# Score matmuls of two heads as 64-row tiles, issued alternately, in place of zero-padded queries

## The chip, the cores and the metric

The kernel runs on one core of a Trainium2 chip. Its time is the device time of one execution, in microseconds (us). A core has five engines that run their own instruction streams and meet at semaphores: TensorE (PE, matrix multiplication, with weight loads shown as PEld), VectorE (DVE), ScalarE (ACT), GpSimd (POOL) and SyncE (SP, here for issuing DMAs). Matmuls write to PSUM, which has 8 banks of 512 float32 columns on 128 partitions.

## The reference, cut to what matters

One layer of a streaming encoder with 1024 prompt tokens and 32 sample tokens: a mixing sub-layer of two head groups, then a SwiGLU feed-forward. The change lies in the mixing sub-layer, in the three places where 64-element queries meet 64-element keys:

```python
# indexer: H_IDX = 8 heads of D_IDX = 64, one shared key
idx = jax.nn.relu(jnp.einsum('bthd,bsd->bths', qi, ki))
score = jnp.einsum('bth,bths->bts', wi, idx)
_, sel = lax.top_k(score, topk)                      # 256 keys per query
# mixer A (band) and mixer B (selected keys): 8 heads of 64
logits = jnp.einsum('bnqhd,bnkhd->bnhqk', q, k) * HEAD_DIM ** -0.5
p = jax.nn.softmax(logits + bias, axis=-1)           # masked
o = jnp.einsum('bnhqk,bnkhd->bnqhd', p, v)
```

Mixer A sees its own chunk and 8 chunks before it (up to 640 keys for a block of 128 queries), mixer B all admissible keys (up to 1024, the sample 1056), of which the indexer's 256 best count. All of it is float32.

## The kernel before, in words

The program is a row of stages, each a block of five engine streams with a barrier behind it: conditioning, projections, `indexer`, `attention(band=True)` (mixer A), `attention(band=False)` (mixer B, with the output projection), then the feed-forward. The change touches `indexer` and the two `attention` stages. In each of them the work is cut into units (t, h): a row block t of 128 queries (t = 0 to 7; t = 8 is the sample with 32 queries) and a head h. A unit's index is u, and in `attention` the program goes by steps s, with unit s scored in step s.

Queries and keys lie transposed, two heads to a tile of 128 partitions: head h has partitions 0 to 63 when h is even, 64 to 127 when it is odd. Keys shared by heads (indexer, mixer B) lie there twice, in both halves. Before the change a score matmul contracts over all 128 partitions. So that the other head adds nothing, POOL copies each unit's query into one of four slots whose other half is zero (`clear_pads`, `fill_pad`, L699), and PE waits for it (`pad_ready`).

`indexer`: PE writes a unit's scores to one of two bank groups (L753) once the unit two before it has been read (L748); ACT applies the relu (L763); DVE multiplies by the head's weight and adds up (L773, L776), and after the last head takes minimum and maximum of the row (L781, L782).

`attention`: in step s PE scores unit s into one of two column ranges of PSUM (L918), once unit s-2 has been masked (L914). DVE adds the near bias (mixer B, L1102) and the mask or band bias with a running minimum (L1110, which raises `masked`); ACT exponentiates (L1001). Two or three steps later PE transposes the weights (L933, a group "T" of up to four blocks) and multiplies with the values (L905, "PV"), reading T's results after ACT or DVE has copied them (L976). When a row block is done, DVE divides by the sums (L1131, at step 8t+8+LAG), PE turns the result (L943, "O"), and in mixer B multiplies with the output weights in two halves of 8 matmuls (L952, "W", at steps 8t+15 and 8t+16); DVE copies W's result (L989), scales it (L1138, at step 8t+19), and POOL adds the residual and stores it (L1163, L1167, L1171). Each engine does its work in program order, so POOL's copies of later queries stand behind its residual work. Beside this DVE carries the search for the top 256: in mixer A a bisection over 24 rounds with counting on DVE (L1063) and ACT (L1011), in mixer B the selection of row block s//8 + 3 in six parts (L1073 to L1085) at steps up to 47.

Of the kernel before, what the change touches and what calls it, by code (L numbers as in the profile page):

```python
# [31 lines left out]
P = 128  # L32
# [4 lines left out]
SAMPLE = NT - 1  # L37
# [44 lines left out]
def rows_of(t):  # L82
    return DEC if t == SAMPLE else P
# [597 lines left out]
def pad_slot(pad, u):  # L681


    return pad + 256 * (u % 2) + P * (u // 2 % 2)


def clear_pads(nc, pool, T, pad, ready):
    nc.gpsimd.memset(T(pad, 256, HD, HD), 0.0).then_inc(ready, 1)
    pool.wait_ge(ready, 1)
    nc.gpsimd.memset(T(pad + 256, 256, HD, 0), 0.0).then_inc(ready, 1)  # L690
    pool.wait_ge(ready, 2)


def fill_pad(nc, pool, T, pad, u, q_at, t, h, used, ready):

    if u >= 4:
        pool.wait_ge(used, u - 3)
    p0, r = HD * (h % 2), rows_of(t)
    nc.gpsimd.tensor_copy(T(pad_slot(pad, u), r, HD, p0), T(q_at + NTOK * (h // 2) + P * t, r, HD, p0)).then_inc(ready, 1)  # L699


def indexer(ctx, nc, ins, outs, sem, T, T3, B, view, ident, d_strip_a, d_strip_b, **_):
# [4 lines left out]
    pad, pad_ready = HT + 7168, sem("pad_ready_i")  # L707
    v_in = sem("v_in")
    EARLY = 24

    def bank(u):
        return 3 * (u % 2)

    with nc.Block() as block:
# [10 lines left out]
        @block.gpsimd  # L725
        def _(pool):
            clear_pads(nc, pool, T, pad, pad_ready)
            for u, (t, h) in enumerate(units[:EARLY]):
                fill_pad(nc, pool, T, pad, u, QI, t, h, idx_mm, pad_ready)
# [10 lines left out]
            for u, (t, h) in enumerate(units[EARLY:], EARLY):  # L740
                fill_pad(nc, pool, T, pad, u, QI, t, h, idx_mm, pad_ready)

        @block.tensor
        def _(pe):
            for u, (t, h) in enumerate(units):
                r = rows_of(t)
                if u >= 2:
                    pe.wait_ge(relu_done, u - 1)  # L748
                pe.wait_ge(pad_ready, u + 3)
                q = T(pad_slot(pad, u), r)  # L750
                for lo, hi in pieces(0, width_b(t), 512):
                    k = T((KI if t < SAMPLE else KIC if lo < PAST else KI + SEQ - PAST) + lo, hi - lo)
                    mm = nc.tensor.matmul(B(bank(u), hi - lo, r, c0=lo), q, k, start=True, stop=True)  # L753
                mm.then_inc(idx_mm, 1)
# [41 lines left out]
def attention(band, ctx, nc, ins, outs, sem, T, T3, B, view, ident, d_ada, d_y, **_):  # L796
# [35 lines left out]
    def key_source(t, h, lo, hi):  # L832

        if band:
            if t == SAMPLE:
                return T(KAC + 512 * (h // 2) + lo, hi - lo) if lo < WIN else T(KA + NTOK * (h // 2) + SEQ + lo - WIN, hi - lo)
            return T(KA + NTOK * (h // 2) + first_key(t) + lo, hi - lo)
        g = h // 4
        if t == SAMPLE:
            return T(KBC + 1024 * g + lo, hi - lo) if lo < PAST else T(KB + NTOK * g + SEQ + lo - PAST, hi - lo)  # L840
        return T(KB + NTOK * g + lo, hi - lo)
# [14 lines left out]

    def s_col(u):
        return 0 if units[u][0] == SAMPLE and not band else 1024 * (u % 2)

    pad = QI + 3168 if band else NAT  # L860
    pad_ready = sem(f"pad_ready_{n}")
# [11 lines left out]
    with nc.Block() as block:  # L873
# [17 lines left out]
        def _(pe):  # L891
# [17 lines left out]
            for s in range(steps):  # L909
                if s < NU:  # L910
                    t, h = units[s]
                    r = rows_of(t)
                    if s >= 2:
                        pe.wait_ge(masked, s if (t == SAMPLE and not band) else s - 1)  # L914
                    pe.wait_ge(pad_ready, s + 3)
                    q = T(pad_slot(pad, s), r)
                    for lo, hi in pieces(0, width(t), 512):
                        mm = nc.tensor.matmul(ps_cols(B, s_col(s) + lo, hi - lo, r), q, key_source(t, h, lo, hi),  # L918
                                              start=True, stop=True)
                    mm.then_inc(qk_mm, 1)  # L920
# [229 lines left out]
        def _(pool):  # L1150
            clear_pads(nc, pool, T, pad, pad_ready)
            for s in range(steps):
                if s < NU:
                    t, h = units[s]
                    fill_pad(nc, pool, T, pad, s, q_at, t, h, qk_mm, pad_ready)
                if band:
                    continue
                for t in range(NT):
                    r = rows_of(t)
                    if s == 8 * t + 8 + 13:  # L1160
                        pool.wait_ge(pad_ready, min(s + 1, NU) + 2)
# [10 lines left out]
            if band:  # L1172
                return
# [380 lines left out]
```

## Time and profile before

| | |
|---|---|
| three timed runs | 1932.95 us median (1930.91 to 1933.37) |
| profiled execution, span of its instructions | 1930.9 us |
| PE busy | 1774.0 us (92%), 9641 matmul records |
| DVE busy | 819.3 us (42%) |
| ACT busy | 651.9 us (34%) |
| POOL busy | 139.4 us (7%) |

The span of the profiled execution equals the lowest of the three runs to a tenth of a microsecond, and lies 2.0 us under their median. Shares of a whole span mix stages with different limits. The stages that the change touches are 435 to 515 us (indexer), 515 to 701 us (mixer A) and 701 to 1071 us (mixer B) of the span; the feed-forward behind them is most of what is left.

### The profile page before, as it was taken

What the parts mean: (1) busy time and instruction counts of PE and PEld (TensorE: products, weight loads), DVE (VectorE), ACT (ScalarE), POOL (GpSimd) and SP (SyncE); (2) the same over time, 40 slices, a digit from 0 to 9 for tenths busy, and PEclk for the clock granted to TensorE, in tenths of its full rate; (3) what the DMA queues carried; (4) which work ended last, traced back from release to release, by engine and by line L of the source; (5) the groups of instructions that cost most, each with busy time, mean ns of one, the idle gap of its engine ahead of it and who ended that gap; (6) DMA issues with size and microseconds to landing.
All of it is one profiled execution on the core that took longest, in us unless ns stands there. A gap on an engine that the chain in (4) does not pass through costs nothing. (4 is left out here: it accounts for less than half of the span.)

```text
span 1930.9 us, 24858 instructions
## 1 busy us (share of the span) xinstructions
PE 1774.0 (92%) x9641; PEld 1436.4 (74%) x9641; DVE 819.3 (42%) x1606; ACT 651.9 (34%) x1188; POOL 139.4 (7%) x273
## 2 busy tenths in 40 slices
PE   7989799999889988899999399999999998999994
PEld 1145499994357865566654299999999998999994
DVE  0120166668899985455433411111111112444446
ACT  1010145545699953233322411111111111333332
POOL 1100000005211011111101100000000000000000
PEclk9999899999899979989999699999999998999997
DMA  9944531113000030000000311111111113200005
GB/s 344 302 80 50 157 77 44 45 35 110 1 1 1 2 134 22 22 22 23 23 23 25 114 56 43 43 44 54 43 43 43 45 42 148 92 0 0 0 0 204
DMA packets 98951, 123.44 MB, mean 64 GB/s; under 512 B 11402, under 2 KB 70866, under 8 KB 98838
## 3 DMA queue, kind: packets, MB, share of 16 engines
q1 hardware_dynamic: 96892, 116.88, 19.8%
q0 software_dynamic: 1984, 5.57, 0.9%
q8 instruction: 46, 0.75, 0.2%
q14 instruction: 29, 0.24, 0.0%
HBM read 105.44 MB, written 18.96 MB: 64 GB/s over the span
## 5 line engine op out<-in xcount | busy, mean ns | idle before, releaser
L1309 PE MATMUL ps<-h_hi,gu_hi 128*128 128x352 f32 x1056 | 341.7, 324 | 8.0 <-DVE gu_lo L1345 8.0
L1309 PE MATMUL ps<-h_lo,gu_hi 128*128 128x352 f32 x1056 | 339.3, 321 | 0.0
L1309 PE MATMUL ps<-h_hi,gu_lo 128*128 128x352 f32 x1056 | 338.9, 321 | 0.0
L918 PE MATMUL ps<-arena 128*128 128x512 f32 (+5 forms) x464 | 181.3, 508 | 35.6 <-DVE small L1110 18.2
L1309 PEld LDWEIGHTS ps<-h_hi,gu_hi 128*128 128x128 f32 x1056 | 198.8, 188 | 8.1 <-DVE gu_lo L1345 8.1
L1309 PEld LDWEIGHTS ps<-h_lo,gu_hi 128*128 128x128 f32 x1056 | 199.1, 189 | 0.0
L1309 PEld LDWEIGHTS ps<-h_hi,gu_lo 128*128 128x128 f32 x1056 | 198.5, 188 | 0.0
L1398 PE MATMUL ps<-a_hi,wd_hi 128*128 128x352 f32 x528 | 174.1, 330 | 13.9 <-DVE a_lo L1421 13.9
L905 PE MATMUL ps<-arena 128*128 128x64 f32 (+2 forms) x1280 | 165.8, 267 | 7.6 <-DVE arena L976 3.2
L1398 PE MATMUL ps<-a_lo,wd_hi 128*128 128x352 f32 x528 | 171.9, 326 | 0.0
L1398 PE MATMUL ps<-a_hi,wd_lo 128*128 128x352 f32 x528 | 171.4, 325 | 0.0
L905 PEld LDWEIGHTS ps<-arena 128*128 128x128 f32 (+2 forms) x1280 | 154.3, 186 | 11.9 <-DVE arena L976 3.6
L918 PEld LDWEIGHTS ps<-arena 128*128 128x128 f32 (+1 forms) x464 | 78.2, 194 | 99.7 <-issue 66.2
L1418 DVE TENSOR_TENSOR wd_lo<-w_down_all,wd_hi 128x1024 fp32r<-128x1024 f32 x66 | 80.8, 1225 | 147.2 <-ACT wd_hi L1410 147.2
L604 PE MATMUL ps<-ht_hi,wb_hi 128*128 128x352 f32 x384 | 128.7, 335 | 12.1 <-DVE ht_lo L641 12.1
L1001 ACT ACTIVATE arena<-arena,small 128x640 f32<-128x640 f32 (+9 forms) x144 | 108.6, 754 | 66.4 <-DVE small L1110 65.9
L1410 ACT CAST wd_hi<-w_down_all 128x1024 fp32r<-128x1024 f32 x66 | 69.1, 1047 | 183.4 <-PE ps L1398 168.0
L952 PE MATMUL ps<-arena 128*128 128x512 f32 (+1 forms) x288 | 127.4, 596 | 0.4 <-ACT arena L983 0.4
L1345 DVE TENSOR_TENSOR gu_lo<-gate_raw,gu_hi 128x1024 fp32r<-128x1024 f32 x22 | 26.9, 1225 | 233.5 <-ACT gu_hi L1323 233.5
L604 PE MATMUL ps<-ht_lo,wb_hi 128*128 128x352 f32 x384 | 125.2, 326 | 0.0
L604 PE MATMUL ps<-ht_hi,wb_lo 128*128 128x352 f32 x384 | 124.8, 325 | 0.0
L976 ACT COPY arena<-ps 128x512 f32<-128x512 f32 (+3 forms) x144 | 66.7, 463 | 169.1 <-PE ps L933 169.0
(172 smaller groups left out, 2611.7 us busy)
## 6 DMA issues: line engine op xcount, KB each, us to landing
arena<-in_w_ada SPq DMA_DIRECT2D x12, 2048.0 KB, 14.0
gate_raw<-in_w_gate SPq DMA_DIRECT2D x22, 512.0 KB, 3.6
up_raw<-in_w_up SPq DMA_DIRECT2D x22, 512.0 KB, 3.7
arena<-in_w_in SPq DMA_DIRECT2D x16, 512.0 KB, 3.5
hidden<-scratch_y SPq DMA_DIRECT2D x4, 2048.0 KB, 12.2
w_down_all<-in_w_down SPq DMA_DIRECT2D x3, 2560.0 KB, 23.6
arena<-in_x_prompt SPq DMA_DIRECT2D x4, 1024.0 KB, 16.1
arena<-in_w_out SPq DMA_DIRECT2D x2, 2048.0 KB, 10.9
```

The costliest lines, as they stand in the source:

```text
L604: mm = nc.tensor.matmul(B(3 * i + c, CH), w_cut[s % 2][a][:, P * i:P * i + P], h_cut[s % 2][b][:, CH * c:CH * c + CH], start=(k == 0 and n ...
L905: mm = nc.tensor.matmul(B(7, HD, r, c0=HD * h), T(pts[t_seq[q] % 4] + P * i, r, k), value_source(t, h, b), start=(b == 0), stop=(b == bloc ...
L918: mm = nc.tensor.matmul(ps_cols(B, s_col(s) + lo, hi - lo, r), q, key_source(t, h, lo, hi), start=True, stop=True)
L952: mm = nc.tensor.matmul(B(bank, 512, r), o, T(W_OUT[c] + 512 * half, 512), start=(c == 0), stop=(c == 7))
L976: copy(view(dst, [[P, len(full)], [1, r]]), view(src, [[P, len(full)], [1, r]])).then_inc(done, 1)
L1001: nc.scalar.activation(T(pbuf[u % NBUF], w, r), T(pbuf[u % NBUF], w, r), ACT.Exp, bias=T(R_NM + u % 16, 1, r), scale=-1.0, accum_out=T(R_S ...
L1309: mm = nc.tensor.matmul(B(3 * i + c, CH), cut[i][a][:, P * k:P * k + P], h[:, NTOK * k + CH * c:NTOK * k + CH * (c + 1)], start=(k == 0 an ...
L1345: nc.vector.tensor_tensor(cut[i][1][:, :], raw[i][:, :], cut[i][0][:, :].bitcast(F32), ALU.subtract).then_inc(cut_lo[i], 1)
L1398: mm = nc.tensor.matmul(B(m, CH), w_cut[k % 2][a][:, P * m:P * m + P], a_cut[k % 2][b][:, :], start=(k == 0 and n == 0), stop=(k == FT - 1 ...
L1410: nc.scalar.copy(w_cut[k % 2][0][:, :], wd[:, D * k:D * k + D]).then_inc(cut_hi, 1)
L1418: nc.vector.tensor_tensor(w_cut[k % 2][1][:, :], wd[:, D * k:D * k + D], w_cut[k % 2][0][:, :].bitcast(F32), ALU.subtract)
```

## The change

POOL's zero-padded slots go. A score matmul contracts over the 64 partitions of its own head, straight from the projected queries. Two heads (h and h+1, one in each half of the partitions) are issued together, one piece of at most 512 columns of the one, then the same piece of the other. The waits change with it: in the indexer a pair has one of two bank groups of 4 banks (for the sample, whose units are wider than 2 banks, a pair waits until every earlier unit is read); in `attention` a pair waits until every earlier unit is masked. The sample of mixer B fills its PSUM columns alone and stays single (`alone`).

```diff
-def clear_pads(...), def fill_pad(...), def pad_slot(...)
+def half_of(h):
+    return HD * (h % 2)
 # indexer
     def bank(u):
-        return 3 * (u % 2)
+        return 3 * (u % 2) if units[u][0] == SAMPLE else 2 * (u % 4)
...
         @block.tensor
-            for u, (t, h) in enumerate(units):
-                if u >= 2:
-                    pe.wait_ge(relu_done, u - 1)
-                pe.wait_ge(pad_ready, u + 3)
-                q = T(pad_slot(pad, u), r)
-                for lo, hi in pieces(0, width_b(t), 512):
-                    mm = nc.tensor.matmul(B(bank(u), hi - lo, r, c0=lo), q, k, start=True, stop=True)
-                mm.then_inc(idx_mm, 1)
+            for u in range(0, len(units), 2):
+                t, h = units[u]
+                if t == SAMPLE:
+                    pe.wait_ge(relu_done, u)
+                elif u >= 4:
+                    pe.wait_ge(relu_done, u - 2)
+                for lo, hi in pieces(0, w, 512):
+                    at = (KI if t < SAMPLE else KIC if lo < PAST else KI + SEQ - PAST) + lo
+                    for i in range(2):
+                        p0 = half_of(h + i)
+                        mm = nc.tensor.matmul(B(bank(u + i), hi - lo, r, c0=lo),
+                                              T(QI + NTOK * (h // 2) + P * t, r, HD, p0), T(at, hi - lo, HD, p0), start=True, stop=True)
+                        if hi == w:
+                            mm.then_inc(idx_mm, 1)
 # attention
+    def alone(u):
+        return units[u][0] == SAMPLE and not band
...
-                if s < NU:
-                    if s >= 2:
-                        pe.wait_ge(masked, s if (t == SAMPLE and not band) else s - 1)
-                    pe.wait_ge(pad_ready, s + 3)
-                    q = T(pad_slot(pad, s), r)
-                    for lo, hi in pieces(0, width(t), 512):
-                        mm = nc.tensor.matmul(ps_cols(B, s_col(s) + lo, hi - lo, r), q, key_source(t, h, lo, hi),
-                                              start=True, stop=True)
-                    mm.then_inc(qk_mm, 1)
+                if s < NU and (alone(s) or s % 2 == 0):
+                    if s:
+                        pe.wait_ge(masked, s)
+                    for lo, hi in pieces(0, w, 512):
+                        for i in range(1 if alone(s) else 2):
+                            q = T(q_at + NTOK * (h // 2) + P * t, r, HD, half_of(h + i))
+                            mm = nc.tensor.matmul(ps_cols(B, s_col(s + i) + lo, hi - lo, r), q, key_source(t, h + i, lo, hi),
+                                                  start=True, stop=True)
+                            if hi == w:
+                                mm.then_inc(qk_mm, 1)
...
         @block.gpsimd
-            clear_pads(nc, pool, T, pad, pad_ready)
+            if band:
+                return
             for s in range(steps):
-                if s < NU:
-                    fill_pad(nc, pool, T, pad, s, q_at, t, h, qk_mm, pad_ready)
                 for t in range(NT):
                     if s == 8 * t + 8 + 13:
-                        pool.wait_ge(pad_ready, min(s + 1, NU) + 2)
                         pool.wait_ge(varm, t + 1)
```

PE in mixer B, row block t = 3 (512 keys), two steps and the start of the third, before (L918 scores, L933 transposes T, L905 values PV):

```order
1966 L918 MATMUL ps<-arena 128x512 [waits pad_ready_b,masked_b]
1967 L933 MATMUL ps<-small,arena 128x128 [waits exp_b,ring_act_b]
1968 L933 MATMUL ps<-small,arena 128x128 x3
1969 L905 MATMUL ps<-arena 128x64 [waits ring_act_b]
1970 L905 MATMUL ps<-arena 128x64 x2
1971 L918 MATMUL ps<-arena 128x512 [waits pad_ready_b,masked_b]
1972 L933 MATMUL ps<-small,arena 128x128 [waits exp_b,ring_dve_b]
1973 L933 MATMUL ps<-small,arena 128x128 x3
1974 L905 MATMUL ps<-arena 128x64 [waits ring_act_b]
1975 L905 MATMUL ps<-arena 128x64 x2
1976 L918 MATMUL ps<-arena 128x512 [waits pad_ready_b,masked_b]
```

The same place after the change (L906 scores, L922 T, L893 PV):

```order
1924 L906 MATMUL ps<-arena 128x512 [waits masked_b]
1925 L906 MATMUL ps<-arena 128x512
1926 L922 MATMUL ps<-small,arena 128x128 [waits exp_b,ring_act_b]
1927 L922 MATMUL ps<-small,arena 128x128 x3
1928 L893 MATMUL ps<-arena 128x64 [waits ring_act_b]
1929 L893 MATMUL ps<-arena 128x64 x2
1930 L922 MATMUL ps<-small,arena 128x128 [waits exp_b,ring_dve_b]
1931 L922 MATMUL ps<-small,arena 128x128 x3
1932 L893 MATMUL ps<-arena 128x64 [waits ring_act_b]
1933 L893 MATMUL ps<-arena 128x64 x2
1934 L906 MATMUL ps<-arena 128x512 [waits masked_b]
1935 L906 MATMUL ps<-arena 128x512
```

The second head's score matmul has moved ahead of one T and PV group, and one wait for the masks stands where two stood. POOL in mixer B, from its copies of queries to the second row block's residual, before:

```order
53 L699 COPY arena<-arena 64x128 [waits qk_mm_b] x18
54 L1163 TENSOR_TENSOR small<-small 128x1 [waits varm,pad_ready_b]
55 L1167 TENSOR_TENSOR arena<-arena 128x1024 [waits xb_in0,m_scaled,rm]
56 L699 COPY arena<-arena 64x128 [waits qk_mm_b,y_done]
57 L699 COPY arena<-arena 64x128 [waits qk_mm_b]
58 L1171 DMA scratch_y<-arena 128x1024 [waits ssy]
59 L699 COPY arena<-arena 64x128 [waits qk_mm_b] x6
```

And after:

```order
34 L1147 TENSOR_TENSOR small<-small 128x1 [waits varm]
35 L1151 TENSOR_TENSOR arena<-arena 128x1024 [waits xb_in0,m_scaled,rm]
36 L1155 DMA scratch_y<-arena 128x1024 [waits ssy,y_done]
37 L1147 TENSOR_TENSOR small<-small 128x1 [waits varm]
38 L1151 TENSOR_TENSOR arena<-arena 128x1024 [waits xb_in1,m_scaled,rm]
```

No copy for PE stands behind POOL's residual work any more.

## Rows read from the trace of the kernel before

**Rows 1.** Stretches of indexer, mixer A, mixer B: length, busy PE, PEld, DVE, ACT, POOL (instructions), clock
```profile
434.90:515.00 80.10, 73.93 (x208) 32.64 (x208) 65.95 (x77) 44.64 (x56) 34.07 (x62) 0.97 0.19 66
515.00:701.00 186.00, 168.82 (x1100) 129.47 (x1100) 166.88 (x597) 166.40 (x370) 20.87 (x74) 0.93 0.00 1
701.00:1071.00 370.00, 341.32 (x1644) 214.08 (x1644) 179.36 (x368) 118.71 (x259) 59.51 (x100) 0.94 0.11 38
```
**Rows 2.** Timeline of the indexer's sample: start, us, engine, line, operation
```profile
497.77 0.11 PEld L753 LDWEIGHTS ps<-arena 128*32 128x32 f32 x1 [0.32 <-issue]
498.20 0.11 PEld L753 LDWEIGHTS ps<-arena 128*32 128x32 f32 x1 [0.32 <-issue]
```
**Rows 3.** Groups by line, DVE, indexer: busy us, mean ns, idle before
```profile
L776 DVE SCALAR_TENSOR_TENSOR tail_attention<-tail_attention,small 128x384 f32<-128x384 f32 (+6 forms) x49 | 49.3, 1006 | 10.0 <-ACT tail_attention L763 6.5
```
**Rows 4.** Groups by line and form, whole span: the indexer's relu and weighting for the sample
```profile
L763 ACT ACTIVATE tail_attention<-ps 32x1056 f32<-32x1056 f32 x8 | 8.3, 1039 | 6.1 <-PE ps L753 5.2 <-DVE tail_attention L773 0.9
L776 DVE SCALAR_TENSOR_TENSOR tail_attention<-tail_attention,small 32x1056 f32<-32x1056 f32 x7 | 9.1, 1306 | 2.1 <-ACT tail_attention L763 1.8
```
**Rows 5.** Timeline of the indexer's start and end
```profile
436.03 4.42 PE L753 MATMUL ps<-arena 128*128 128x384 f32 x8 [2.77 <-POOL arena L699]
438.24 0.42 DVE L773 TENSOR_SCALAR tail_attention<-tail_attention,small 128x384 f32<-128x384 f32 x1 [3.09 <-ACT tail_attention L763]
513.58 1.23 DVE L782 TENSOR_REDUCE small<-tail_attention 32x1 f32<-32x1056 f32 x1
```
**Rows 6.** Groups by line, DVE, mixer A: the copies that wait for PE
```profile
L976 DVE COPY arena<-ps 128x128 f32<-128x128 f32 x32 | 9.2, 288 | 4.2 <-PE ps L933 4.0
```
**Rows 7.** A stretch of mixer A with 640 keys, columns as in Rows 1
```profile
600.00:650.00 50.00, 49.89 (x352) 40.87 (x351) 45.46 (x155) 46.25 (x94) 5.22 (x18) 1.00 0.00 1
```
**Rows 8.** Waits in mixer B from 726 us: total us, times, longest
```profile
PE ps L918 <- POOL arena L699: 9.3, 4, 3.9
```
**Rows 9.** Timeline of mixer B, row block 2, units 21 and 22
```profile
752.54 3.00 POOL L1167 TENSOR_TENSOR arena<-arena 128x1024 f32<-128x1024 f32 x1 [1.45 <-issue]
756.39 0.43 DVE L1102 TENSOR_TENSOR ps<-ps,arena 128x256 f32<-128x256 f32 x1
756.65 1.62 PE L918 MATMUL ps<-arena 128*128 128x384 f32 x2 [3.88 <-POOL arena L699]
756.86 0.56 DVE L1110 CUSTOM_DVE_ANT_0 arena<-ps,tail_attention 128x384 f32<-128x384 f32 x1
763.08 7.12 PE L952 MATMUL ps<-arena 128*128 128x512 f32 x16
```
**Rows 10.** Timeline of mixer B, row block 7, one step and the next one's start
```profile
961.46 1.94 PE L918 MATMUL ps<-arena 128*128 128x512 f32 x4
963.24 0.60 PE L933 MATMUL ps<-small,arena 128*128 128x128 f32 x4
963.67 1.00 PE L905 MATMUL ps<-arena 128*128 128x64 f32 x8
965.79 1.94 PE L918 MATMUL ps<-arena 128*128 128x512 f32 x4
967.77 0.43 DVE L1102 TENSOR_TENSOR ps<-ps,arena 128x256 f32<-128x256 f32 x1 [1.92 <-PE ps L918]
968.23 1.22 DVE L1110 CUSTOM_DVE_ANT_0 arena<-ps,tail_attention 128x1024 f32<-128x1024 f32 x1
```
**Rows 11.** Short stretches of mixer A and B, columns as in Rows 1
```profile
536.00:540.00 4.00, 1.89 (x10) 1.36 (x11) 3.83 (x14) 3.71 (x11) 0.29 (x1) 1.00 0.00 0
752.00:756.00 4.00, 0.77 (x7) 0.53 (x6) 3.93 (x6) 1.56 (x5) 3.39 (x2) 1.00 0.00 0
756.00:760.00 4.00, 3.35 (x12) 2.66 (x13) 2.82 (x8) 2.79 (x7) 2.34 (x6) 0.54 0.33 129
```
**Rows 12.** Timeline of mixer B's sample: matmuls over 32 rows between ones over 128
```profile
1013.70 0.29 PE L905 MATMUL ps<-arena 32*32 32x64 f32 x2
1013.92 0.20 PE L933 MATMUL ps<-small,arena 32*32 32x32 f32 x1
1014.05 0.64 PE L905 MATMUL ps<-arena 128*32 128x64 f32 x8
```

More of the change, by code:

```diff
@@ L678 @@
 BIAS_A, BIAS_B = HT, HT + 5120
[L681 to L699, printed above, removed]
+def half_of(h):
+    return HD * (h % 2)
 def indexer(ctx, nc, ins, outs, sem, T, T3, B, view, ident, d_strip_a, d_strip_b, **_):
@@ L706, in indexer @@
     relu_at = [X + 5280, X + 5280 + 1056]
-    pad, pad_ready = HT + 7168, sem("pad_ready_i")
     v_in = sem("v_in")
-    EARLY = 24
     def bank(u):
-        return 3 * (u % 2)
+        return 3 * (u % 2) if units[u][0] == SAMPLE else 2 * (u % 4)
     with nc.Block() as block:
@@ L726, in _ @@
         def _(pool):
-            clear_pads(nc, pool, T, pad, pad_ready)
-            for u, (t, h) in enumerate(units[:EARLY]):
-                fill_pad(nc, pool, T, pad, u, QI, t, h, idx_mm, pad_ready)
             pool.wait_ge(bias_in, 32)
@@ L739, in _ @@
             nc.gpsimd.memset(T(R_M01 + 192, 64, 64), BIG).then_inc(edge_done, 1)
-            for u, (t, h) in enumerate(units[EARLY:], EARLY):
-                fill_pad(nc, pool, T, pad, u, QI, t, h, idx_mm, pad_ready)
         @block.tensor
         def _(pe):
-            for u, (t, h) in enumerate(units):
-                r = rows_of(t)
-                if u >= 2:
-                    pe.wait_ge(relu_done, u - 1)
-                pe.wait_ge(pad_ready, u + 3)
-                q = T(pad_slot(pad, u), r)
-                for lo, hi in pieces(0, width_b(t), 512):
-                    k = T((KI if t < SAMPLE else KIC if lo < PAST else KI + SEQ - PAST) + lo, hi - lo)
-                    mm = nc.tensor.matmul(B(bank(u), hi - lo, r, c0=lo), q, k, start=True, stop=True)
-                mm.then_inc(idx_mm, 1)
+            for u in range(0, len(units), 2):
+                t, h = units[u]
+                r, w = rows_of(t), width_b(t)
+                if t == SAMPLE:
[10 more added lines that the diff above has]
+                            mm.then_inc(idx_mm, 1)
         @block.scalar
@@ L835, in key_source @@
             if t == SAMPLE:
[L836 to L841, printed above, removed]
+                at = KAC + 512 * (h // 2) + lo if lo < WIN else KA + NTOK * (h // 2) + SEQ + lo - WIN
+            else:
+                at = KA + NTOK * (h // 2) + first_key(t) + lo
+        elif t == SAMPLE:
+            at = KBC + 1024 * (h // 4) + lo if lo < PAST else KB + NTOK * (h // 4) + SEQ + lo - PAST
+        else:
+            at = KB + NTOK * (h // 4) + lo
+        return T(at, hi - lo, HD, half_of(h))
     def value_source(t, h, b):
@@ L855, in block_rows @@
         return min(P, width(t) - P * b)
+    def alone(u):
+        return units[u][0] == SAMPLE and not band
     def s_col(u):
         return 0 if units[u][0] == SAMPLE and not band else 1024 * (u % 2)
-    pad = QI + 3168 if band else NAT
-    pad_ready = sem(f"pad_ready_{n}")
     if band:
@@ L909, in _ @@
             for s in range(steps):
-                if s < NU:
+                if s < NU and (alone(s) or s % 2 == 0):
                     t, h = units[s]
-                    r = rows_of(t)
-                    if s >= 2:
-                        pe.wait_ge(masked, s if (t == SAMPLE and not band) else s - 1)
-                    pe.wait_ge(pad_ready, s + 3)
-                    q = T(pad_slot(pad, s), r)
-                    for lo, hi in pieces(0, width(t), 512):
-                        mm = nc.tensor.matmul(ps_cols(B, s_col(s) + lo, hi - lo, r), q, key_source(t, h, lo, hi),
-                                              start=True, stop=True)
-                    mm.then_inc(qk_mm, 1)
+                    r, w = rows_of(t), width(t)
+                    if s:
[7 more added lines that the diff above has]
+                                mm.then_inc(qk_mm, 1)
                 for j, it in enumerate(plan[s]):
@@ L1150, in _ @@
         def _(pool):
-            clear_pads(nc, pool, T, pad, pad_ready)
+            if band:
+                return
             for s in range(steps):
-                if s < NU:
-                    t, h = units[s]
-                    fill_pad(nc, pool, T, pad, s, q_at, t, h, qk_mm, pad_ready)
-                if band:
-                    continue
                 for t in range(NT):
@@ L1171, in _ @@
                         pool.dma_start(d_y[P * t:P * t + r, :], T(XB[t % 2], D, r)).then_inc(y_out[t % 2], 16)
-            if band:
-                return
             pool.wait_ge(y_out[0], 16 * (NT // 2 + 1))
```

## The prediction

> **What bounds the kernel now.** I read the stretches of the three touched stages first, because the page's shares mix them with stages that this change leaves alone. In the indexer PE is busy 73.9 of 80.1 us, DVE 66.0; in mixer A the three engines are close together (PE 168.8, DVE 166.9, ACT 166.4 of 186.0); in mixer B PE is busy 341.3 of 370.0 and DVE 179.4 [rows 1]. So PE sets the pace in the indexer and in most of mixer B, and in mixer A a faster PE meets two engines that are nearly as full.
>
> Next, what a score matmul costs. The program has 104 of them in the indexer and the trace 208 records [rows 1]: each float32 matmul is two. Two weight loads of 512-column records lie 0.43 us apart [rows 2], so a matmul over 512 columns costs 0.85 us at the 2.4 GHz level, whatever number of its 128 rows is zeros. The recorded 0.6 us durations overlap; I use starts. The indexer's score matmuls cover 8 x 5280 columns: 70 us, nearly all of PE's time there.
>
> Then the waits. PE waits for POOL's padded copies 9.3 us in four places of mixer B [rows 8]; one of them is unit 22, which starts at 756.65 after 3.88 us idle, because POOL first had to add the residual (3.00 us from 752.54) [rows 9]. At each stage's start PE also waits for the slots to be cleared and filled (2.77 us idle before 436.03 [rows 5], of which about 1.0 lies behind the barrier).
>
> **What the change does to a pair of heads.** If the two row halves of the array work at the same time, head h+1 can run its first record while head h runs its second. A pair then costs the columns of one head plus one record of its first piece: for 1024 columns 1.71 + 0.43 = 2.13 us where it was 3.41, for 896 1.92 instead of 2.99, for 640 1.49 instead of 2.13, for 384 0.96 instead of 1.28. No row of this trace has two matmuls on different row groups, so the bounds are this and no gain at all (0.43 us per record, one after the other). I take overlap, because every operand it needs is there in both halves and the two heads write to different banks; that is the main uncertainty.
>
> The Trainium skill, page "TensorE: Matmul & The Clock Gate", section "Measured speedup vs the span model", has 3.07 times for four row tiles, not 4, and none for float32. As an estimate from it two tiles would give about 1.5 times, which in the sums below costs some 3 us. No run here shows it yet.
>
> **Indexer: 6 us less.** With scores at half price (some 35 us, four bank groups ahead) DVE is next: 65.95 us busy [rows 1], in a chain where each accumulation waits for the one before. Its idle before them is 10.0 us, 6.5 of it for ACT, which waits for PE [rows 3]. I keep 2.2 us of small gaps (about 0.04 in each of 55 steps). DVE's first work is at 438.24, 2.2 us after PE's first at 436.03 [rows 5]; without the slots PE starts about 1.0 us earlier, so DVE begins at 437.2. The sample goes the other way: its pair waits until all relus before it are done. A round is then the first head's scores (1.8 us at hand), two relus of 1.04 [rows 4] and wake-ups, about 4.0 us, where two accumulations of 1.31 take DVE 2.7 [rows 4]; over the last three rounds that is 3.4 us lost, while the first hides behind row block 7's minimum and maximum. 437.2 + 65.95 + 2.2 + 3.4 = 508.8, against 514.8 (513.58 + 1.23 [rows 5]): 6.0 us. Bounds: 9.5 if the sample's rounds hide, a loss of 6 if nothing overlaps (below).
>
> **Mixer A: 2 us less.** POOL's 18 copies in 50 us give the step: 2.78 us, with DVE busy 45.5 and ACT 46.3 [rows 7], so they need 2.5 and 2.6 a step at the very least, and their small semaphore gaps come on top. What DVE really lost to PE is the 4.2 us before its copies [rows 6]. A pair now waits until every earlier unit is masked; but DVE has copying and counting behind each mask for longer than the first head's 1.07 us, so its queue covers the new latency. I take 1 us of the 4.2 and the 1.0 us at the start. Bounds: nothing, and 5.
>
> **Mixer B: 6 us less.** In four parts.
> - Start: 1.1 us less, as PE no longer waits for slots.
> - Row blocks 0 and 1 (128 and 256 keys): DVE paces. It now finds the next pair's scores late when the selecting part behind the mask is shorter than the scores take: up to 0.4 us a pair (128 columns at the 1.2 GHz level are 0.43 us), over eight pairs some 2 us more.
> - Row blocks 2 to 5: the trap. POOL's stalls go, but not the time. Unit 22 may now start only when unit 21 is masked: bias at 756.39, mask 0.56 us from 756.86 [rows 9], done about 757.45, which is 0.8 us later than the 756.65 that POOL allowed. Then both heads come in 0.96 us and two T and PV groups of 3 blocks follow. From Rows 10, four transposes take 0.43 us (963.24 to 963.67) and the four blocks' PV 0.85, so a group of three is 0.97. At full clock the W matmuls would start at 760.4 instead of 763.08 [rows 9], 2.7 us earlier. But PE idles about as long ahead of it as it does now, and the clock fell to half (0.54) after such a gap: PE was busy 0.77 of 4 us, then came the slow stretch [rows 11]. At 1.2 GHz the same work ends at 763.3: no gain. In block 5, where the selecting parts are longest, the stricter wait costs up to 1 us even at full clock. I take 1 us less for the four together. Bounds: the 9.3 us of stalls and four pairs' saving in each block (4 x (0.32 + 0.43 + 0.64 + 0.85) = 9) at the one end, 3 us more per block at the other.
> - Row blocks 6 and 7: nothing but masks on DVE, and PE is busy all the time. A step of block 7 is 4.33 us (961.46 to 965.79) of which scores 1.78 [rows 10]; a pair goes from 8.66 to about 7.4. DVE, from the first head's end: bias 0.43, mask 1.22 [rows 10], a copy of 0.69 and the second mask, 6.2 us after the pair's start, so PE doesn't wait. Three pairs in each block save 1.07 and 1.28; the first, which has the W matmuls between its heads, 0.4 and 0.8; one pair in each loses 0.5 because DVE waits for PV of the block before: 7.3 us. Each pair also changes between 64-row and 128-row matmuls twice. Nearest rows: two 32-row PV records take 0.22 us and a 32-row transpose 0.13 (1013.70, 1013.92, 1014.05 [rows 12]), against 0.11 for records over 128 rows in block 7: at most about 0.1 us a change, 1.6 us for the 8 pairs. Net 5.7. Bounds: nothing, and 9.5.
>
> Together -1.1 + 2 - 1 - 5.7 = -5.8. The sample (single heads) stays as it is.
>
> A rule that speaks against the change: the Trainium skill, "TensorEngine Tiling (Array Packing)", section "Key Properties", says that a change of tiling mode drains TensorE. The 32-row rows agree so far as they show a price of this size, no more; without that price the sum would be 1.6 us lower.
>
> POOL's 200 copies (34 us in the indexer [rows 1]) cost nothing where PE didn't wait for them, and their going gains nothing there.
>
> **Sum.** 6.0 + 2.0 + 5.8 = 14 us off the profiled 1930.9. That execution is 2.0 us under the median of the runs, so I set it against 1932.95: **1919 us**.
>
> **The rivals.**
> 1. *The heads don't overlap* (slower). The two heads' records then run one after the other, and interleaving makes the first head finish late, by one or two pieces of the second, while the wait for masks or relus is stricter than before. Indexer: prompt blocks as now, the sample's round 3.56 + 2 x 1.04 + 0.1 = 5.7 us instead of 3.56, four times 2.1, less the 1.0 at the start and what hides: +6. Mixer A: -1. Mixer B: starts -1.1, blocks 0 and 1 +2, blocks 2 to 5 +1 with the later first head, 6 and 7 +1.5 and 1.6 for mode changes: about +5. Together some +10: **1943 us**. It decides if a pair costs more than about 1.8 times a head. For it: no row shows overlap. Against it: nothing shares a partition or a bank.
> 2. *Waiting pairs cool the clock.* PE with gaps of 2 to 3 us behind each pair stays at 1.2 GHz in blocks 2 to 5 (3 us more each than taken, 7 to 10 in all). Against it: a stretch with PE busy 1.89 of 4 us kept full clock [rows 11], and the indexer would have that share. Time: about **1928 us**.
> 3. *The clock holds instead* in blocks 2 to 5 and their W matmuls start 2 to 3.5 us earlier each, with DVE's lost waits in mixer A regained: 12 us more, **1907 us**. For it: with both heads at once the work behind the gap is shorter. Against: the gaps remain.
>
> **Chances.** Forecast 0.56, overlap missing 0.17, cool clock 0.15, holding clock 0.12. Within 0.2% (3.9 us: what a measurement here can tell from no change) ends at 1929.1 and 1936.8; about half of rival 2's spread falls in it. Faster 0.75, same 0.09, slower 0.16. The forecast alone: 1912 to 1925. For 8 in 10 I go to 1904 below, and up to 1934, which leaves out most of the serial case.
>
> **What would show it.** Overlap: score records of a pair with starts half a record apart or two at a time, and the indexer's PE busy share near half with DVE at 90% or more. Indexer's end near 509, its sample in rounds of 4 us. Mixer A's step near 2.7. In mixer B no wait on POOL, but PE idle for L1110's masks before pairs of blocks 2 to 5, and pairs of block 7 every 7.4 us. I am wrong if these pairs take 8.6 us, if the indexer still lasts 80, or if the granted clock sits at half through whole row blocks.

## The result, and the profile after

The changed kernel takes **1969.22 us** (median of 4 runs, 1965.49 to 1972.46) against 1932.94 for the kernel before: ratio 1.0189, 95% interval 1.0173 to 1.0204. It is 36 us slower; I had predicted 14 us faster, and the time lies far outside my range. The profiled span is 1968.0 us (1930.9 before), its mean granted clock 0.919 (0.955). Of all executions behind the tables below, one of e10 (4474 us) and one of e11 (9469 us) stand far above the others; no trace shows why, and the ratios leave them out.

The stages of [rows 1] in the changed kernel, where each takes longer, so that the stretches are longer too: length, busy PE, PEld, DVE, ACT, POOL (instructions), granted clock, DMA share, GB/s.

```profile
434.90:516.00 81.10, 49.68 (x208) 16.98 (x204) 65.28 (x76) 43.99 (x56) 1.50 (x4) 0.84 0.19 65
517.00:725.00 208.00, 163.05 (x1102) 126.53 (x1104) 166.19 (x594) 167.11 (x370) 0.00 (x0) 0.80 0.00 1
725.00:1105.00 380.00, 340.24 (x1644) 209.48 (x1644) 178.36 (x367) 119.73 (x259) 31.39 (x24) 0.86 0.10 37
```

The clock column is the news: .84, .80 and .86 where it was .97, .93 and .94. In the indexer PE's busy time did fall from 73.9 to 49.7 us, yet the stage ends no earlier. Between the first masks of the stages and row blocks named:

| us | before | changed | predicted |
|---|---|---|---|
| span's start to mixer A | 517.0 | 517.6 (+0.6) | -6.0 |
| mixer A (row blocks 1 to 3 of it) | 186.5 (51.9) | 208.3 (69.7): +21.8 | -2.0 |
| mixer B, row blocks 0 to 7 | 285.1 | 282.5 (-2.6) | -5.8 |
| mixer B's sample to the span's end | 942.3 | 959.6 (+17.3) | 0 |

The four differences make 37.1 us, the difference of the spans. Of mixer A's 21.8 us, 17.9 lie in row blocks 1 to 3, 2.5 in row blocks 4 to 7 and 1.4 in its sample. The sample of mixer B is the plainest place: TensorE busy all the time, at 1.2 GHz.

```profile
1030.00:1070.00 40.00, 40.00 (x173) 20.98 (x172) 11.57 (x27) 9.18 (x18) 3.49 (x3) 0.50 0.05 17
```

The heads do overlap. Two pairs of mixer B's row block 7 and what follows them (timeline: start, us, engine, line, operation, number of records; L922 are transposes, L932 turns the result, L941 are the output weights W):

```profile
984.27 1.99 PE L906 MATMUL ps<-arena 64*128 64x512 f32 x8
986.19 0.66 PE L922 MATMUL ps<-small,arena 128*128 128x128 f32 x4
991.37 0.61 PE L932 MATMUL ps<-small,tail_attention 128*128 128x128 f32 x4
991.91 1.99 PE L906 MATMUL ps<-arena 64*128 64x512 f32 x8
999.01 7.08 PE L941 MATMUL ps<-arena 128*128 128x512 f32 x16
```

Eight records, two heads, in 1.99 us, where one head took 1.94 [rows 10]. From the first score to the transposes behind it are 1.92 us (984.27 to 986.19), where one head took 1.78 [rows 10]. The second pair and its four T and PV groups take 7.10 us (991.91 to 999.01), where two steps took 8.66; between the two pairs lie 7.64 us, because the turning of the result stands there too (0.54 us from 991.37), which the two steps of [rows 10] don't hold. The Trainium skill's "TensorE: Matmul & The Clock Gate", section "Measured speedup vs the span model", has 3.07 times for four row tiles, from which two tiles would give about 1.5 times as an estimate; the trace shows 1.85 (two heads at 1.78 us each against 1.92 for the pair), and the measurement decides.

The indexer's sample, which answers to the 4.0 us rounds of the prediction: PE's four pairs, the wait before each in brackets.

```profile
490.51 3.73 PE L734 MATMUL ps<-arena 64*32 64x512 f32 x12 [2.78 <-ACT tail_attention L746]
496.30 3.63 PE L734 MATMUL ps<-arena 64*32 64x512 f32 x12 [2.05 <-ACT tail_attention L746]
501.98 2.68 PE L734 MATMUL ps<-arena 64*32 64x512 f32 x12 [2.06 <-ACT tail_attention L746]
506.71 3.54 PE L734 MATMUL ps<-arena 64*32 64x512 f32 x12 [2.05 <-ACT tail_attention L746]
```

A round is 3.7 us of scores and 2.05 us of waiting for the relus, 5.7 us together (the third has scores of 2.68 us; its clock was higher for a while). DVE's weighting (busy as in [rows 3]) now waits 13.6 us, 8.5 of it for ACT:

```profile
L759 DVE SCALAR_TENSOR_TENSOR tail_attention<-tail_attention,small 128x384 f32<-128x384 f32 (+6 forms) x49 | 49.1, 1002 | 13.6 <-ACT tail_attention L746 8.5 <-DVE tail_attention L759 0.5
```

Mixer A's row blocks 1 to 3, before and then changed, and the changed kernel's wait for masks there (total us, times, longest):

```profile
530.30:582.20 51.90, 43.09 (x248) 30.99 (x248) 48.94 (x183) 50.49 (x122) 6.92 (x24) 0.99 0.00 1
```
```profile
531.00:600.70 69.70, 51.39 (x242) 37.15 (x242) 48.90 (x182) 53.72 (x127) 0.00 (x0) 0.65 0.00 1
```
```profile
PE ps L906 <- DVE small L1099: 16.7, 9, 2.8
```

DVE does the same 48.9 us of work; PE is idle 18.3 us instead of 8.8, and slow besides. Two causes are possible: PE waits for the pair's masks, or its clock is low. In mixer B from 748 us the waits for POOL's copies [rows 8] are gone, and this one stands there:

```profile
PE ps L906 <- DVE small L1099: 22.8, 12, 4.0
```

### The profile page after: what moved, and what is told of

Read it like the earlier page. It is cut to its first block and busy times, and to the rows that moved or that the text cites. A ratio compares the mean times of both kernels' runs of the same rounds, so it can differ in the third digit from the quotient of the medians.

```text
span 1968.0 us, 24449 instructions
## 1 busy us (share of the span) xinstructions
PE 1742.7 (89%) x9641; PEld 1413.5 (72%) x9641; DVE 819.1 (42%) x1606; ACT 653.2 (33%) x1188; POOL 59.0 (3%) x67
## 5 line engine op out<-in xcount | busy, mean ns | idle before, releaser
L893 PE MATMUL ps<-arena 128*128 128x64 f32 (+2 forms) x1280 | 183.1, 287 | 9.3 <-ACT arena L965 5.2
L906 PE MATMUL ps<-arena 64*128 64x512 f32 (+5 forms) x464 | 119.8, 580 | 77.2 <-DVE small L1099 69.9
L893 PEld LDWEIGHTS ps<-arena 128*128 128x128 f32 (+2 forms) x1280 | 171.5, 203 | 15.2 <-ACT arena L965 7.2
L906 PEld LDWEIGHTS ps<-arena 64*128 64x128 f32 (+1 forms) x464 | 45.0, 204 | 130.9 <-DVE small L1099 78.4
L1392 ACT CAST wd_hi<-w_down_all 128x1024 fp32r<-128x1024 f32 x66 | 69.1, 1048 | 183.5 <-PE ps L1380 168.1
L941 PE MATMUL ps<-arena 128*128 128x512 f32 (+1 forms) x288 | 129.1, 602 | 0.4 <-ACT arena L972 0.4
```

The source lines that it names most:

```text
L893: mm = nc.tensor.matmul(B(7, HD, r, c0=HD * h), T(pts[t_seq[q] % 4] + P * i, r, k), value_source(t, h, b), start=(b == 0), stop=(b == bloc ...
L906: mm = nc.tensor.matmul(ps_cols(B, s_col(s + i) + lo, hi - lo, r), q, key_source(t, h + i, lo, hi), start=True, stop=True)
L941: mm = nc.tensor.matmul(B(bank, 512, r), o, T(W_OUT[c] + 512 * half, 512), start=(c == 0), stop=(c == 7))
L1392: nc.scalar.copy(w_cut[k % 2][0][:, :], wd[:, D * k:D * k + D]).then_inc(cut_hi, 1)
```

## The experiments

Theory 1: scores over 64 rows don't hold TensorE's full clock. Theory 2: the clock falls because overlap leaves gaps. Theory 3: the pair's stricter wait costs the time. In the kernels PAIRED holds the row blocks (8 is the sample) whose heads go two at a time, WIDE those with padded queries over 128 rows; a head that goes singly waits as in the kernel before. The changed kernel is

```
PAIRED = {'i': {2, ..., 8}, 'a': {0, ..., 8}, 'b': {0, ..., 7}}
WIDE = {'i': set(), 'a': set(), 'b': set()}
```

The stages of all runs, from their profiles, in us: the indexer's prompts (first relu to the last memset) and sample; mixer A's row blocks 1 to 3 and whole; mixer B's row blocks 0 to 7, and its sample from its first mask to its last. Medians are of the timed executions, ratios against executions of the kernel before taken in the same round; the stages are those of the profiled execution alone.

| kernel | median (ratio, 95%) | i prompts, sample | A 1-3, all | B 0-7, sample |
|---|---|---|---|---|
| before | 1932.9 | 62.7, 14.4 | 51.9, 186.5 | 285.1, 41.0 |
| changed | 1969.2 (1.0173-1.0204) | 59.3, 21.9 | 69.7, 208.3 | 282.5, 54.6 |
| e1 | 1963.4 (1.0139-1.0173) | 59.3, 29.3 | 69.1, 207.6 | 282.6, 41.0 |
| e2 | 2093.9 (1.0802-1.0894) | 60.3, 13.2 | 80.7, 323.4 | 295.4, 55.1 |
| e3 | 1998.5 (1.0316-1.0350) | 64.4, 26.4 | 72.2, 226.1 | 295.4, 39.3 |
| e4 | 1989.2 (1.0282-1.0325) | 59.3, 21.9 | 65.6, 204.5 | 278.6, 49.1 |
| e5 | 1955.1 (1.0084-1.0123) | 59.3, 22.0 | 54.5, 200.1 | 277.3, 54.7 |
| e6 | 1923.8 (0.9930-0.9964) | 59.4, 18.0 | 51.9, 186.5 | 278.1, 39.3 |
| e7 | 1918.6 (0.9902-0.9935) | 60.3, 13.2 | 52.0, 186.6 | 273.6, 41.0 |
| e8 | 1925.4 (0.9944-0.9972) | 59.4, 17.9 | 52.0, 186.5 | 279.9, 41.0 |
| e9 | 1977.3, one run | 59.3, 27.9 | 70.8, 209.3 | 281.7, 55.7 |
| e10 | 1927.2 (0.9949-0.9976) | 60.3, 13.2 | 51.9, 186.5 | 282.5, 40.9 |
| e11 | 1942.4 (1.0033-1.0059) | 60.3, 13.2 | 65.5, 204.5 | 273.8, 41.0 |
| e12 | 1967.4, one run | 59.3, 18.5 | 67.1, 205.5 | 285.6, 54.6 |

**e1: the samples over 128 rows.**
```diff
-WIDE = {'i': set(), 'a': set(), 'b': set()}
+WIDE = {'i': {8}, 'a': set(), 'b': {8}}
```


> The changed kernel, with the scores of the sample's row block in the indexer and in mixer B taken over 128 rows again, one head after the other, from queries padded with zeros (the same instructions as in the kernel before there); everything else, mixer A included, as changed. Theory 1 (matmuls on 64 rows don't hold TensorE's full clock): the indexer's sample falls from 21.9 us to about 14.4, and in mixer B's sample the 40 us at a granted clock of .50 come back to about 1.00 and 20 us; together 1969 - 7.5 - 16.7 = 1945 us, range 1940 to 1950, mixer A's 208 us unchanged. Theory 2 (the clock falls where TensorE has gaps, since two heads now overlap): in mixer B's sample nothing overlaps and TensorE has no gaps in either, so that stretch stays at .50 and 40 us; only the indexer's 7.5 us come back: 1962 us. Theory 3 (the stricter wait of a pair costs the time): no wait of mixer B's sample differs, so 1962 us as well.

In mixer B theory 1 holds: the same single heads over 128 rows, and the stretch that answers to the one at .50 above runs at .97; the sample takes 41.0 us instead of 54.6.

```profile
1040.00:1080.00 40.00, 40.00 (x254) 21.80 (x253) 13.13 (x34) 10.73 (x22) 3.91 (x5) 0.97 0.05 17
```

Where the clock falls is the same in both kernels: PE waits 1.20 us for DVE early in the sample, and the scores behind this wait run at half clock. Before, and then changed (a row of L918 or L906 is one head's scores; the changed kernel's heads between those shown take 3.73 us too):

```profile
1008.40 0.61 PE L905 MATMUL ps<-arena 128*32 128x64 f32 x8 [1.20 <-DVE tail_attention L1131]
1008.84 3.64 PE L918 MATMUL ps<-arena 128*32 128x512 f32 x6
1014.52 1.94 PE L918 MATMUL ps<-arena 128*32 128x512 f32 x6
```
```profile
1028.23 0.61 PE L893 MATMUL ps<-arena 128*32 128x64 f32 x8 [1.20 <-DVE tail_attention L1120]
1028.77 3.73 PE L906 MATMUL ps<-arena 64*32 64x512 f32 x6
1036.04 3.73 PE L906 MATMUL ps<-arena 64*32 64x512 f32 x6
1066.16 8.88 PE L941 MATMUL ps<-arena 128*128 128x512 f32 x16
```

With padded queries one head later the clock is back; with 64 rows it stays at .50 until the 16 matmuls of W over 128 rows (1.00 from 1070 us on). The indexer's part was not what the expectation says: its padded heads still went as pairs, with the pair's wait and without overlap, and took 29.3 us. So this run leaves the indexer open, and its total, 1963.4, is near the 1962 of theories 2 and 3 only because the indexer's loss (7.4 us) hides half of mixer B's gain.

**e2: single heads over 64 rows.**
```diff
-PAIRED = {'i': {2, ..., 8}, 'a': {0, ..., 8}, 'b': {0, ..., 7}}
+PAIRED = {'i': set(), 'a': set(), 'b': set()}
```


> The order and all waits of the kernel before (one head after the other), but each head's scores over its own 64 rows, without padded queries, in all three stages. Theory 1 (64 rows don't hold the full clock): TensorE's work per head is that of before, at a clock of about .5 in the indexer's sample, in mixer A's row blocks 1 to 3 and in mixer B's sample, and perhaps in the whole indexer: slower than the changed kernel's 1969 us, 1975 to 2030, and mixer A's row blocks 1 to 3 take over 70 us (51.9 in the kernel before, 69.7 in the changed one). Theory 2 (gaps from the overlap) and theory 3 (the pair's wait): without overlap and without the pair's wait the time is that of the kernel before, 1928 to 1938 us, clock .95.

Far slower than I thought possible. Mixer A at 64 rows, and the kernel before over as many records:

```profile
440.00:500.00 60.00, 58.18 (x176) 26.02 (x176) 53.89 (x66) 37.58 (x49) 1.50 (x4) 1.00 0.23 81
560.00:820.00 260.00, 260.00 (x891) 186.75 (x890) 122.45 (x419) 124.17 (x252) 0.00 (x0) 0.50 0.00 1
```
```profile
560.00:690.00 130.00, 127.95 (x891) 99.86 (x890) 119.47 (x410) 120.39 (x250) 12.21 (x45) 1.00 0.01 1
```

891 records take 260 us at .50, never idle, and 130 us at 1.00. Gaps (theory 2) and the pair's wait can't be what keeps the clock down, since neither is there. It fell ahead of mixer A, as in the kernel before, whose first row block runs at .50 too and whose second at .98. The first row limits theory 1: in the indexer's prompts 64-row scores keep 1.00, though heads that follow each other lie in different halves and partly overlap there. In mixer B of the same run nothing overlaps, and they keep it as well once it is back:

```profile
862.00:866.00 4.00, 4.00 (x13) 2.71 (x13) 0.96 (x5) 1.65 (x6) 0.00 (x0) 0.50 0.02 4
864.77 8.40 PE L1005 MATMUL ps<-arena 128*128 128x512 f32 x16
866.00:870.00 4.00, 4.00 (x8) 1.55 (x8) 0.00 (x0) 0.00 (x0) 0.00 (x0) 0.82 0.00 0
950.00:1150.00 200.00, 199.35 (x984) 124.90 (x982) 98.33 (x180) 68.31 (x127) 16.16 (x12) 1.00 0.06 22
```

It came back in W's 16 matmuls over 128 rows (L1005), which mixer A doesn't have. So 64-row scores of single heads hold a full clock; what they didn't do is win it back.

**e3: pairs over 128 rows.**
```diff
-WIDE = {'i': set(), 'a': set(), 'b': set()}
+WIDE = {'i': {2, ..., 8}, 'a': {0, ..., 8}, 'b': {0, ..., 8}}
```


> The order and the waits of the changed kernel (two heads issued alternately, one wait for the pair), but each head's scores over 128 rows from queries padded with zeros, so that no two matmuls overlap. Theory 1 (64 rows don't hold the full clock): granted clock .95 again, mixer A's row blocks 1 to 3 at 52 to 60 us, mixer B's sample at 80 us to its end; 1930 to 1945 us in all. Theory 3 (the pair's wait): the 17.8 us of mixer A's row blocks 1 to 3 stay and grow by the matmuls that don't overlap, 1955 to 1975 us; only mixer B's sample, where heads go singly, comes back. Theory 2 (gaps from the overlap) expects what theory 1 expects.

Slower than all three forecasts. The pair's order and wait, without overlap, cost mixer A 20.3 us in row blocks 1 to 3 (clock .74, so a wait too lowers it) and 3 to 4 us in each later one, where the changed kernel's overlap pays it back. Theory 3 holds for mixer A; mixer B's sample, over 128 rows, is back (39.3).

**e4: useless 128-row work.**
```diff
+for i in range(2 if (band and 1 <= t <= 3) or (not band and t == SAMPLE) else 0):
+    nc.tensor.matmul(B(bank, P), ident[:, :], ident[:, :], start=True, stop=True)
```
Two such matmuls stood there, not the one of the expectation.

> The changed kernel with useless work: ahead of the transposes of each ring item of mixer A's row blocks 1 to 3 (24 items) and of mixer B's sample (24 items and some partial ones) one more matmul of 128 rows by 128 columns, into a bank that the transposes then overwrite; about .43 us each at full clock, so some 10 us of work in each of the two places. Theory 1 (what counts is how many rows of the array work, and the cool clock is what costs): the granted clock rises from .50-.72 in row blocks 1 to 3 and from .50 in the sample, and the time falls in spite of the added work, by 10 to 25 us to 1945 to 1960. Theory 3 (waits, not the clock): the time grows by 5 to 30 us, 1974 to 2000. If the added rows are too few to raise the clock, the time grows as well, and the granted clock stays: then this run says nothing against theory 1.

The profiled execution took 1960.2 us at a mean granted clock of 0.940, the four others 1988 to 1998 at 0.919 to 0.925; why is open. The median, 1989.2, lies where the expectation put theory 3, so the total decides nothing for theory 1, and only stages of the profiled execution are read here. Mixer A's row blocks 1 to 3, and mixer B's sample:

```profile
532.50:598.10 65.60, 50.51 (x327) 40.43 (x327) 48.77 (x183) 51.84 (x124) 0.00 (x0) 0.88 0.00 1
1024.00:1064.00 40.00, 40.00 (x272) 25.10 (x269) 12.26 (x28) 9.45 (x19) 3.50 (x3) 1.00 0.05 18
```

In the sample more work takes less time (49.1 us, 54.6 without it): the clock was the cost. In mixer A .65 becomes .88, and only 4.1 us of the 17.8 come back. Even these are not sure: the changed kernel's mixer A, untouched in e1, e9, e11 and e12, took 69.1, 70.8, 65.5 and 67.1 us there.

**e5: four places for scores.**
```diff
-return 0 if units[u][0] == SAMPLE and not band else 1024 * (u % 2)
+if units[u][0] == SAMPLE and not band:
+    return 0
+return 512 * (u % 4) if width(units[u][0]) <= 512 else 1024 * (u % 2)
...
 # pairs of at most 512 keys
-pe.wait_ge(masked, s)
+pe.wait_ge(masked, s - 2)
```


> The changed kernel with four one-bank places for scores in row blocks of at most 512 keys (row blocks 0 to 3 of both mixers), so that a pair waits for the masks of the pair before last (masked >= s-2) and not for those of the last one; same matmuls on 64 rows, same order. Theory 3 (the pair's wait costs mixer A's row blocks 1 to 3 their time): they fall from 69.7 us to 50 to 56 us (51.9 in the kernel before), and mixer B's row blocks 1 to 3 from 103.4 to about 97; 1940 to 1952 us in all, whatever the granted clock. Theory 1 (64 rows don't hold the clock, and the cool clock is the cost): row blocks 1 to 3 stay at 64 to 70 us at a granted clock of .50 to .72; 1962 to 1970 us in all. Mixer B's sample is not touched: 40 us at .50 by both.

```profile
532.50:587.00 54.50, 45.31 (x234) 33.10 (x233) 48.74 (x183) 50.84 (x123) 0.00 (x0) 0.72 0.00 1
```
```profile
PE ps L975 <- DVE small L1168: 2.0, 1, 2.0
```

Theory 3 for mixer A: without the wait (16.7 us down to 2.0) 15.2 of the 17.8 us come back, though the clock is still .72; PE idles 9.2 us, as in the kernel before (8.8). The whole, 1955.1, is above the 1940 to 1952 expected, mainly because row block 4, the first with two places again, takes 28.2 us instead of 21.8; its clock is .70, where the changed kernel had .97, and why is not shown.

**e9 and e12: the indexer's sample.** Useless 128-row matmuls, two ahead of each pair's scores (e9), or six behind them, in the wait (e12):
```diff
+for i in range(6 if t == SAMPLE else 0):
+    nc.tensor.matmul(B(7, P), ident[:, :], ident[:, :], start=True, stop=True)
```


> The changed kernel with two useless matmuls of 128 rows by 128 columns ahead of each pair of the indexer's sample (8 in all, overwritten afterwards); nothing else differs. The pair's wait is the same. Theory 1 (the cool clock is what made the rounds 5.7 us long): the granted clock of the sample's rounds rises from .52 to .8 or more, and a round takes 4 to 5 us in spite of the added .9 us, the sample 16 to 19 us (21.9 in the changed kernel). Theory 3 (the pair's wait makes the round, whatever the clock), or the clock not raised by so little: rounds of 6.6 to 7.4 us, the sample 26 to 30 us.

> The changed kernel with six useless matmuls of 128 rows by 128 columns behind each pair of the indexer's sample, into a bank that nothing reads, so that they lie in the 2.05 us in which TensorE waits for ScalarE's relu, and not ahead of the scores. Theory 1 (the cool clock makes the rounds of 5.7 us: 3.7 us of scores at half clock and 2.05 us of waiting): with TensorE busy throughout the clock rises from .50 to .8 or more by the third round, a round then takes 1.9 + 2.05 = 3.9 to 4.3 us, and the sample 16 to 19 us. Theory 3 (the wait alone makes the round, whatever the clock): rounds of 5.7 us or more at whatever clock. If the clock stays at .50, the six take 3.7 us at half clock, a round takes 7.4 us, and the sample 28 us: then 128-row work on 128 columns between the scores isn't enough to lift it.

In e9 the clock stayed at .50 and a round took 6.9 us, so by its expectation e9 can't tell the theories apart. In e12 the clock rose:

```profile
491.35 3.73 PE L789 MATMUL ps<-arena 64*32 64x512 f32 x12 [2.94 <-ACT tail_attention L802]
495.02 2.67 PE L793 MATMUL ps<-small 128*128 128x128 f32 x12
497.61 1.97 PE L789 MATMUL ps<-arena 64*32 64x512 f32 x12
501.63 1.97 PE L789 MATMUL ps<-arena 64*32 64x512 f32 x12 [0.52 <-ACT tail_attention L802]
505.66 1.97 PE L789 MATMUL ps<-arena 64*32 64x512 f32 x12 [0.52 <-ACT tail_attention L802]
```
```profile
500.00:505.00 5.00, 4.48 (x34) 2.93 (x33) 2.90 (x3) 2.95 (x4) 0.00 (x0) 1.00 0.00 0
```

Scores 1.97 instead of 3.73 us, a round 4.03 (501.63 to 505.66) under the same wait: the 4.0 of the prediction, at full clock.

**e6, e7, e8, e10, e11: what is worth keeping.** All have mixer A as before and mixer B's sample over 128 rows, save e11, whose mixer A is the changed one; e8 is e6 with e5's four places.
```diff
-WIDE = {'i': {8}, 'a': {0, ..., 8}, 'b': {0, 1, 2, 3, 8}}
+WIDE = {'i': set(), 'a': {0, ..., 8}, 'b': {0, 1, 2, 3, 8}}
-PAIRED = {'i': {2, ..., 7}, 'a': set(), 'b': {4, 5, 6, 7}}
+PAIRED = {'i': set(), 'a': set(), 'b': {4, 5, 6, 7}}
```
(from e6 to e7; e10 has no pairs at all and is wide throughout both mixers; e11 is e7 with all of 'a' in PAIRED and none in WIDE.)

> Each stage in the form that the runs so far show cheapest for it: in the indexer pairs over 64 rows for the prompts and single padded heads for the sample; mixer A as in the kernel before (single heads, 128 rows, padded); mixer B as before in row blocks 0 to 3 and in the sample, pairs over 64 rows in row blocks 4 to 7. Theory (64 rows lower the clock only where TensorE is also short of work or short of columns, and the pair's wait costs where rounds are short): indexer 73 us from its first relu (77.1 before, 81.2 changed), mixer A 186 as before, mixer B's row blocks 4 to 7 at 167 us (177.5 before), sample as before; 1933 - 4 - 10 = 1919 us, range 1914 to 1924. Rival (the clock carries over: the pairs of row blocks 4 to 7 leave it low for the sample, or the indexer's prompts for mixer A): 1930 to 1950 us.

> As the run before it, but in the indexer all heads singly over 64 rows, without pads (the form in which the run of single heads over 64 rows took 73.5 us from its first relu). Theory: the same as the run before within 2 us, 1917 to 1921, so what the indexer needs is not overlap but no pads and no pair's wait; mixer A starts at a granted clock of .50 and is lifted by its matmuls on 128 rows, as the kernel before lifts it from .72. Rival (128-row matmuls can't lift it in mixer A's short row blocks): row blocks 1 to 3 of mixer A at over 60 us, 1930 or more.

> The first mix, with four one-bank places for scores in the row blocks of at most 512 keys of both mixers (a single head waits for the mask three heads back, not one). If TensorE's wait for the masks is what holds mixer B's row blocks 0 to 3 (107.4 us before) they fall by 3 to 8 us, and mixer A's row block 1 to 3 (51.9) stay, since VectorE and ScalarE are busy there for 18.5 to 19.7 us of 20: 1911 to 1917 us. If the wait doesn't hold them, the first mix's time, 1919 us.

> The second mix (indexer single heads over 64 rows, mixer A as before, mixer B as before save pairs over 64 rows in row blocks 4 to 7), without those pairs: both mixers as in the kernel before, the indexer alone changed to single heads over 64 rows without pads. If the overlap of two heads is worth in mixer B's row blocks 4 to 7 what the traces say (9 to 12 us), 1928 to 1931 us; if the second mix's gain came from the indexer alone, 1918 to 1922.

> The second mix with mixer A alone in the changed form (pairs over 64 rows, the pair's wait). If the pair's wait and the clock in mixer A cost what the changed kernel shows, mixer A takes 206 to 210 us (186.5 in the kernel before) and the whole 1938 to 1942 us; if that cost came from what the indexer's sample left behind (a clock already low when mixer A began), 1920 to 1928 us.

e7 beats both kernels: 0.8% below the one before. Its indexer needs no pairs: single heads over 64 rows without pads take 73.5 us there, 77.1 in the kernel before, 77.4 in e6. Taking its pairs out of mixer B (e10) costs 8.7 us; putting them into mixer A (e11) costs 23.9 between the medians and 17.9 in mixer A itself (204.5, a little under the 206 to 210 expected), though mixer A's first row block begins at the same half clock in both. e6 is at its upper edge: its sample (18.0 us) waits once for all relus at the change of banks. e8, which expected 1911 to 1919, gains nothing: mixer B's row blocks 0 to 3 take 107.6 us, 107.5 in the kernel before. But its clock in row blocks 2 and 3 was .85 and .83, and .95 and .91 in e6, so whether the mask wait holds them stays open.

## Why the prediction was wrong

- **"The sample (single heads) stays as it is"**: the step that failed most plainly. I counted order and instructions there, and both stayed; the clock did not. It cost 13.7 us to the last mask and 17.3 to the end, and e1, which in mixer B changes only the rows of the sample's scores, takes the 13.7 back.
- **Mixer A, "its queue covers the new latency"**: -2.0 became +21.8. DVE is covered, but I asked only who waits for scores, not what stands behind the waiting pair on PE: transposes and PV, whose results ACT and DVE copy. e5 shows that the wait is the larger part (15.2 of 17.8 us in row blocks 1 to 3); the clock is the smaller (4.1 in e4, within what the same code differs by from run to run); they overlap, since e3's wait lowers the clock too. That the queue behind the pair is the path, I argue from the timeline; no run takes it alone. My rival 2 had a part of this, waiting pairs that cool the clock, but in mixer B's row blocks 2 to 5, and at 9 us.
- **Indexer, "about 4.0 us" a round**: right in form and at full clock (e12: 4.03); at half clock 5.7. The prompts gained 3.4 us, and the sample lost 7.5, where I had priced its loss at 3.4 (three rounds of 4.0 us against 2.7 are 3.9 by my own numbers).
- **Mixer B's row blocks**: 6 and 7 gave 8.3 us, where I had 5.7; 0 and 1 lost 4.0 (I had 2), 2 to 5 lost 1.7 (I had a gain of 1). Together -2.6, not -5.8.
- **Overlap** was right, and the serial rival wrong. It was larger than I priced it: I had the second head one record (0.43 us) behind the first, but both run at once, so a pair of row block 7 took 7.10 us, where 7.4 was forecast without mode changes. 8.66 less one head's scores (1.78 us) would be 6.88; the 0.22 us left over agree with the 0.2 a pair that I priced for the mode changes. Against 7.6 with the mode changes that is 0.5 us a pair, enough for what row blocks 6 and 7 gave beyond the forecast.
- My closing sentence named what came: "the granted clock sits at half through whole row blocks". I argued against it from one stretch that had kept its clock with a half-idle PE [rows 11], a stretch of 128-row work.

## What to carry to other kernels

A new form of a matmul can cost the clock even where order and number of instructions stay: read the granted clock of every stretch that the form touches, the ones with an unchanged order too, look for the gap behind which it falls and for what brings it back, and price each stretch at both levels. When two heads share one wait, look at what is queued behind it on TensorE. Here pairs paid where TensorE sets the pace and rounds are long (mixer B's row blocks of 640 keys and more); in mixer A, where DVE and ACT are nearly as full, its row blocks of 640 keys lost 2.5 us by them. Keep single heads, or more places, where rounds are short. Test a change stage by stage: the parts kept in e7 are worth 14 us against the kernel before, and the changed kernel is 50 us behind e7.

## What the runs showed of the hardware

Scores of single heads over 64 rows kept the full clock when they had it (e2's mixer B, PE busy 199.35 of 200 us, 1.00), but where it had fallen a fully busy TensorE with transposes and PV among them sat at 0.50 for 260 us (e2's mixer A); with padded queries as many records ran at 1.00. Behind a gap of 1.20 us in mixer B's sample the clock fell in both forms; padded scores had it back one head later, 64-row ones only with W's 16 matmuls over 128 rows. The Trainium skill, "TensorE: Matmul & The Clock Gate", section "What's actually happening", has the clock follow how busy TensorE is; busy 260.00 of 260.00 us at 1.2 GHz differs from that, if the profile's busy time is what the page means, and the measurement decides. Useless 128-row matmuls brought the clock back in mixer B's sample (e4, 1.00) and in the indexer's (e12, 24 of them, 1.00); the eight of e9 left it at 0.50. Two heads over 64 rows each, in different halves, run at once: 8 records in 1.99 us, where 4 took 1.94.
